# Values, probabilities and p of the first block turned by VectorE in 32x32 squares and placed by DMA, instead of turned by TensorE

## What is computed

```python
hn = rmsnorm(h, norm1[i]);  z = hn @ w_in[i]
u, q, k, v = ...                              # 256 + 3 x 768 features
q, k = rotary(q), rotary(k)                   # 12 heads of 64
# three head groups of 4 heads, dilation 1, 4 and 16, blocks of 128 queries
s = q_block @ k_block(s).T * 64 ** -0.5       # own block and, where there is one, the block before
e = exp(s - max);  o = (e @ v) ...            # the groups' shares are applied later
h = h + concat(pool(u), o) @ w_out[i]
h = h + square(relu(rmsnorm(h, norm2[i]) @ w_up[i])) @ w_down[i]
gate = sigmoid(rmsnorm(h, norm3[i]) @ w_gate[i])
h = h + gate * (p[i] @ w_ple[i])              # p[i]: 1024 tokens x 256
```

## Time and profile before

| | |
|---|---|
| time, median of 3 runs (lowest, highest) | 3045.55 us (3045.34, 3045.76) |
| span of the profiled execution | 3043.6 us |
| PE busy | 3025.0 us, 99% of the span |
| DVE, ACT, POOL busy | 69%, 35%, 64% |
| mean busy share of the 16 DMA engines on queues q1 (SP), q10 (ACT) | 24.0%, 7.3% |

### The profile page before, as it was taken

One profiled execution on the slowest core, in us unless ns is written; L12 is line 12 of the kernel. 1 busy time (PEld: TensorE's weight loads), 2 busy tenths in 40 slices (PEclk: granted clock), 3 DMA queues, 4 the chain that ended last, 5 costly groups with the idle time before them and its releaser, 6 DMA issues.

```text
span 3043.6 us, 40003 instructions
## 1 busy us (share of the span) xinstructions
PE 3025.0 (99%) x14420; PEld 2448.4 (80%) x14420; DVE 2085.4 (69%) x2848; ACT 1057.5 (35%) x1911; POOL 1951.7 (64%) x1630
## 2 busy tenths in 40 slices
PE   8999999999999999999999999999999999999999
PEld 7777888888888888778888888888888777788887
DVE  6656585556888865565665558888769988797223
ACT  4223253333444421233343334444331345302112
POOL 5632458888999557433558878998545544486574
PEclk9999999999999999999999999999999999999999
DMA  5112234446444221112144456544111100111112
GB/s 167 51 42 50 74 108 160 152 153 246 154 152 166 82 84 51 48 43 87 50 140 153 152 187 213 154 148 151 47 44 49 35 28 22 32 49 49 46 63 83
DMA packets 367379, 301.71 MB, mean 99 GB/s; under 512 B 66640, under 2 KB 302160, under 8 KB 365648
## 3 DMA queue, kind: packets, MB, share of 16 engines
q1 hardware_dynamic: 318432, 222.33, 24.0%
q10 hardware_dynamic: 48752, 76.83, 7.3%
HBM read 223.29 MB, written 72.68 MB: 97 GB/s over the span
## 4 chain that ended last, share of the span: by engine, by line
PE 97%; DVE 2%; ACT 0%; issue 0%; DMA 0%; SPq 0%; DVEq 0%; ACTq 0%
PE ring L1581 14%; PE ring L1583 14%; PE ring L1582 14%; PE ring L1862 4%; PE ring L1863 4%; PE ring L1864 4%; PE ring L1895 4%; PE ring L1897 4%; PE ring L1896 4%; PE aux L1581 3%; PE aux L1583 3%; PE aux L1582 3%; PE aux L1895 2%; PE aux L1897 2%; PE aux L1896 2%; PE aux L1862 2%
## 5 line engine op out<-in xcount | busy, mean ns | idle before, releaser
L1288 POOL TENSOR_TENSOR w_hi<-w_raw,ones_r 128x512 fp32r<-128x512 f32 (+3 forms) x296 | 326.4, 1103 | 589.9 <-PE ring L1583 516.5
L1291 POOL TENSOR_TENSOR w_lo<-w_raw,w_hi 128x512 fp32r<-128x512 f32 (+3 forms) x296 | 382.5, 1292 | 23.2
L1581 PE MATMUL ring<-Q_hi,w_hi 128*128 128x512 f32 x752 | 300.1, 399 | 0.0
L1583 PE MATMUL ring<-Q_hi,w_lo 128*128 128x512 f32 x752 | 293.3, 390 | 0.0
L1582 PE MATMUL ring<-Q_lo,w_hi 128*128 128x512 f32 x752 | 293.0, 390 | 0.0
L1581 PE MATMUL ring<-P_hi,w_hi 128*128 128x512 f32 x656 | 268.2, 409 | 1.6 <-DVE P_lo L2716 1.2
L1583 PE MATMUL ring<-P_hi,w_lo 128*128 128x512 f32 x656 | 256.3, 391 | 0.0
L1582 PE MATMUL ring<-P_lo,w_hi 128*128 128x512 f32 x656 | 256.0, 390 | 0.0
L3211 DVE SCALAR_TENSOR_TENSOR conv_out<-conv_in,taps,conv_out 128x1021 f32<-128x1021 f32 (+29 forms) x120 | 188.0, 1614 | 0.2
L1581 PEld LDWEIGHTS ring<-Q_hi,w_hi 128*128 128x128 f32 x752 | 141.1, 188 | 54.0 <-issue 26.3
L1583 PEld LDWEIGHTS ring<-Q_hi,w_lo 128*128 128x128 f32 x752 | 141.2, 188 | 30.2
(11 more groups left out here) (494 smaller groups left out, 8536.5 us busy)
## 6 DMA issues: line engine op xcount, KB each, us to landing
hid_scratch<-stages SPq DMA_DIRECT2D x196, 256.0 KB, 2.1
w_raw<-in_w_in SPq DMA_DIRECT2D x84, 512.0 KB, 3.9
w_raw<-in_w_down SPq DMA_DIRECT2D x64, 512.0 KB, 3.8
p_slot<-hid_scratch ACTq DMA_DIRECT2D x50, 512.0 KB, 4.7
q_slot<-hid_scratch ACTq DMA_DIRECT2D x48, 512.0 KB, 4.7
w_raw<-in_w_up SPq DMA_DIRECT2D x36, 512.0 KB, 4.8
up_raw<-in_w_up SPq DMA_DIRECT2D x28, 512.0 KB, 5.2
p_slot<-first_scratch ACTq DMA_DIRECT2D x12, 1024.0 KB, 7.3
```

What stands on the lines that cost most here:

```text
L1288: g.tensor_tensor(w_hi[:, slot, ks], w_raw[:, slot, ks], one.broadcast_to([P, width, P]), ALU.mult).then_inc(w_hi_ready, 1)
L1291: g.tensor_tensor(w_lo[:, slot, ks], w_raw[:, slot, ks], w_hi[:, slot, ks].bitcast(F32), ALU.subtract).then_inc(w_ready, 1)
L1581: t.matmul(o, wh, xh, start=first, stop=False)
L1583: return t.matmul(o, wl, xh, start=False, stop=last)
```

## The change

VectorE's transpose works on squares of 32x32 only. The change does each transposition in two steps. DVE turns every 32x32 square in place of itself; then DMA puts each square where it belongs.

- Probabilities: `take_scores` and `exp_block` now work in the PSUM banks `turned`. A new job "send" stands five chunks (`SEND_LAG`) behind each step: DVE transposes both banks into `probs` (two instructions of 128x512), and ACT issues one DMA of `probs` (512 KB, rows of 4 KB) to DRAM. At the next step ACT, behind `take_attended` and ahead of `exp_block`, waits for that DMA to land and for `attended` of the stop before, and issues four DMAs (`fetch_probs`), each of 32 partitions by 32 pieces of 32 elements (128 bytes), from DRAM to `probs_t`. PE's `attend` waits for them (`probs_back`).
- Values: DVE transposes `v_feat` in itself (128x1024) where PE's first `turn_v` stood; ACT sends it to DRAM, and at step 0 of the unit, as the first thing, fetches it with four such DMAs to `v_t`.
- p: SP loads it in eight DMAs of 64 KB for each half, again in pieces of 128 bytes, so that the squares stand in the right place before they are turned; DVE transposes 128x512 four times in a layer, in `add_plain`.
- PE's transposes for all three, ACT's copies of v and p and DVE's copies of the probabilities go. Some semaphores are merged.

The core of the diff:

```diff
-STEPS, LAG = 8, 2
+STEPS, LAG, SEND_LAG = 8, 2, 5
+SQUARES = 4
...
-        put(m0, 1, "turn_v", unit, 0)
-        put(m0, 4, "turn_v", unit, 1)
+        put(m0, 1, "turn_v", unit)
...
+            put(m0 + (k + SEND_LAG) // KC, (k + SEND_LAG) % KC, "send", unit, i)
...
     for i in range(stops_of(5) + LAG):
         put_a(8 + 8 * i, "step", 5, i)
+        if i < stops_of(5):
+            put_a(8 + 8 * i + SEND_LAG, "send", 5, i)
...
# SP
-            sp.dma_start(p_raw[:], p_d[l][:, 4 * hf:4 * hf + 4]).then_inc(p_loaded, 16)
+            for i in range(4):
+                for c in range(2):
+                    sp.dma_start(p_raw[32 * i:32 * i + 32, c], p_d[l][hf, c, i]).then_inc(p_loaded, 16)
...
# PE
-            for unit, i in parts:
-                if 1 <= i <= stops_of(unit):
-                    for j in blocks_of(unit, i - 1):
-                        turn_probs(l, unit, j)
...
# PE, attend
-            pe.wait_ge(probs_taken, no + 1)
+            pe.wait_ge(probs_back, 16 * SQUARES * (stops_before(l, unit, j * stops_of(unit) // STEPS) + 1))
...
+            if j == 0:
+                pe.wait_ge(v_back, 16 * SQUARES * (l * UNITS + unit + 1))
...
# ACT
+        def send_v(l, unit):
+            act.wait_ge(v_turned, l * UNITS + unit + 1)
+            act.dma_start(v_d[unit % 2], v_feat[:]).then_inc(v_sent, 16)
+
+        def fetch_v(l, unit):
+
+            act.wait_ge(v_sent, 16 * (l * UNITS + unit + 1))
...
+            squares = v_d[unit % 2].rearrange("(a t) (j b i) -> b t j a i", a=SQUARES, j=8, b=SQUARES)
+            for b in range(SQUARES):
+                act.dma_start(v_t[unit % 2][32 * b:32 * b + 32].rearrange("t j (a i) -> t j a i", a=SQUARES), squares[b]).then_inc(v_back, 16)
...
+        def send_probs(l, unit, i):
+            no = stops_before(l, unit, i)
+            act.wait_ge(probs_turned, step_no(l, unit, blocks_of(unit, i)[-1]) + 1)
+            act.dma_start(probs_d[no % 2], probs[:].rearrange("q x e k -> q (x e k)")).then_inc(probs_sent, 16)
+
+        def fetch_probs(l, unit, i):
+
+            no = stops_before(l, unit, i)
+            act.wait_ge(probs_sent, 16 * (no + 1))
+            act.wait_ge(attended, step_no(l, unit, blocks_of(unit, i)[0]))
+            squares = probs_d[no % 2].rearrange("(a t) (x b j) -> b t x a j", a=SQUARES, b=SQUARES, j=32)
+            for b in range(SQUARES):
+                to = probs_t[32 * b:32 * b + 32].rearrange("t x e k -> t (x e k)").rearrange("t (x a j) -> t x a j", a=SQUARES, j=32)
+                act.dma_start(to, squares[b]).then_inc(probs_back, 16)
+
+        def attention_stop(l, parts):
+            for unit, i in parts:
+                if i >= 2:
+                    for j in blocks_of(unit, i - 2):
+                        take_attended(l, unit, j)
+            for unit, i in parts:
+                if 1 <= i <= stops_of(unit):
+                    fetch_probs(l, unit, i - 1)
+            for unit, i in parts:
+                if i < stops_of(unit):
+                    for j in blocks_of(unit, i):
+                        exp_block(l, unit, j)
...
# DVE
+        def turn_v(l, unit):
+            dve.wait_ge(half_free, half_no(l, 4 + 3 * unit, 1) + 1)
+            v.transpose(v_feat[:], v_feat[:]).then_inc(v_turned, 1)
+
+        def turn_probs(l, unit, i):
+
+            blocks = blocks_of(unit, i)
+            dve.wait_ge(exped, 2 * step_no(l, unit, blocks[-1]) + 2)
+            dve.wait_ge(probs_sent, 16 * stops_before(l, unit, i))
+            for x in range(2):
+                mm = v.transpose(probs[:, x].rearrange("q e k -> q (e k)"), turned[x])
+            mm.then_inc(probs_turned, len(blocks))
...
+        def turn_p(l, c, hf):
+
+            dve.wait_ge(p_loaded, 16 * 8 * (2 * l + hf + 1))
+            if hf:
+                dve.wait_ge(p_ready, p_no(l, c, 0) + 1)
+            v.transpose(p_turned[:, c], p_raw[:, c].rearrange("p j f -> p (j f)")).then_inc(p_copied, 1)
```

More of the change, by code:

```diff
@@ L243, with stops_before @@
 HN3_AFTER = {DOWNS - 4: (0,), DOWNS - 3: (1, 2), DOWNS - 2: (3, 4), DOWNS - 1: (5, 6)}
-STEPS, LAG = 8, 2
+STEPS, LAG, SEND_LAG = 8, 2, 5
+SQUARES = 4
 def stops_of(unit):
     return 2 if unit % GROUPS == 2 else 4
+def stops_before(l, unit, i):
+    return sum(stops_of(u) for u in range(UNITS)) * l + sum(stops_of(u) for u in range(unit)) + i
 def unit_parts(unit, i):
@@ L806, in two_blocks @@
     rooted = sem("rooted")
-    v_taken = sem("v_taken")
+    v_turned = sem("v_turned")
+    v_sent = sem("v_sent")
+    v_back = sem("v_back")
     exped = sem("exped")
-    probs_taken = sem("probs_taken")
+    probs_sent = sem("probs_sent")
+    probs_back = sem("probs_back")
     attn_taken = sem("attn_taken")
@@ L1014, in stat_no @@
         return STATS * l + 2 * i + hf
-    def v_no(l, unit, b):
-        return 2 * (UNITS * l + unit) + b
     def step_no(l, unit, s):
@@ L1497, in _ @@
         for e in range(2):
-            g.memset(left[:, e, 0:1], 1.0).then_inc(left_made, 1)
+            g.memset(left[:, e, 0:1], 1.0).then_inc(keep_made, 1)
         def mask_shares(c, r):
@@ L1638, in sum_split @@
             t.matmul(side, ones_r[:], sum_lo[:, cols], start=False, stop=True).then_inc(side_done, 1)
-        def turn_v(l, unit, b):
-            side_starts(l, "turn_v", unit, b)
-            pe.wait_ge(half_free, half_no(l, 4 + 3 * unit, 1) + 1)
-            for j in range(4):
-                mm = t.transpose(side[:, j * P:j * P + P], v_feat[:, (4 * b + j) * P:(4 * b + j) * P + P], ident[:])
-            mm.then_inc(side_done, 1)
-        def turn_probs(l, unit, j):
-            g, no, (buf, at) = unit % GROUPS, step_no(l, unit, j), buffer_of(unit, j)
-            pe.wait_ge(exped, 2 * no + 2)
-            if stops_of(unit) == 4 and no >= 2:
-                pe.wait_ge(probs_taken, no - 1)
-            elif first_of_stop(unit, j):
-                pe.wait_ge(probs_taken, no)
-            for e in range(2):
-                for b in range(2 if has_prev(g, j) else 1):
-                    mm = t.transpose(turned[buf][:, 256 * e + at + b * P:256 * e + at + b * P + P], probs[:, buf, e, at + b * P:at + b * P + P], ident[:])
-            mm.then_inc(probs_turned, 1)
         def attend(l, unit, j):
@@ L1725, in spread @@
             t.matmul(side, sel[:, g], rows[:], start=True, stop=True).then_inc(side_done, 1)
-        def turn_p(l, c, hf):
-            side_starts(l, "turn_p", c, hf)
-            pe.wait_ge(p_loaded, 16 * (2 * l + hf + 1))
-            for b in range(4):
-                mm = t.transpose(side[:, b * P:b * P + P], p_raw[:, b, c * P:c * P + P], ident[:])
-            mm.then_inc(side_done, 1)
         def woven(l, m, k):
@@ L1940, in _ @@
             turn_x(i)
-        pe.wait_ge(eps_made, 1)
+        pe.wait_ge(ones_made, 2)
         for l in range(DEPTH):
@@ L2251, in exp_block @@
             n, (buf, at) = 2 * P if has_prev(g, j) else P, buffer_of(unit, j)
-            act.wait_ge(max_ready, step_no(l, unit, j) + 1)
+            act.wait_ge(max_ready, step_no(l, unit, j | 1 if stops_of(unit) == 2 else j) + 1)
             for e in range(2):
-                x_ = probs[:, buf, e, at:at + n]
+                x_ = turned[buf][:, 256 * e + at:256 * e + at + n]
                 a.activation(x_, x_, ACT.Exp, scale=SCALE, bias=neg_max[:, j % 4, e:e + 1],
@@ L2312, in woven @@
                 elif kind == "turn_v":
-                    take_v(l, *args)
+                    send_v(l, *args)
                 elif kind == "step":
-                    for part in unit_parts(*args):
-                        attention_stop(l, *part)
+                    if args[1] == 0:
+                        fetch_v(l, args[0])
+                    attention_stop(l, unit_parts(*args))
+                elif kind == "send":
+                    send_probs(l, *args)
                 elif kind == "pool":
@@ L2786, in take_v @@
             if unit and hf == 0:
-                dve.wait_ge(side_done, side_no(l, "turn_v", unit - 1, 1) + 1)
+                dve.wait_ge(v_sent, 16 * (l * UNITS + unit))
             dve.wait_ge(half_done, no + 1)
@@ L2812, in take_scores @@
             dve.wait_ge(attn_consts, l + 1)
+            dve.wait_ge(probs_turned, step_no(l, unit, blocks_of(unit, s * stops_of(unit) // STEPS)[0]))
             dve.wait_ge(scored, step_no(l, unit, last_of_stop(unit, s)) + 1)
             for e in range(2):
-                v.tensor_tensor_reduce(out=probs[:, buf, e, half:half + n], in0=scores[e][:, col:col + n], in1=m, scale=1.0, scalar=-3.0e38,
+                v.tensor_tensor_reduce(out=turned[buf][:, 256 * e + half:256 * e + half + n], in0=scores[e][:, col:col + n], in1=m, scale=1.0, scalar=-3.0e38,
                                        op0=ALU.add, op1=ALU.max, accum_out=row_stat[:, unit, s, e:e + 1]).then_inc(masked, 1)
@@ L2873, in woven @@
                     invert(l, 2, args[0])
+                elif kind == "turn_v":
+                    turn_v(l, *args)
                 elif kind == "step":
```

(5 more changed lines are left out.)

92 lines of the change are left out of this document (27 added, 65 removed).

## The result

The changed kernel takes 3097.7 us (median of four runs, 3096.9 to 3099.4) against 3045.5 us (3045.3 to 3045.8) before: ratio 1.017, 95% interval 1.0158 to 1.0183. Slower by 52 us, where 10 us less had been forecast (3035), and outside the range of 3005 to 3095. The profiled execution has a span of 3095.6 us, so 52.0 more than that of before.

The account below looks back on a forecast made before the run. TensorE, busy 99% of the span, was taken to bound the kernel: span 3043.6 - 48 saved + 37 of waits = 3032.6, plus 1.95 from span to median, about 3035 us; range 3005 to 3095, forecast's own 3017 to 3039.

Parts of the forecast that it names:

- What TensorE saves: Transposes removed from TensorE: 34.0 us for probabilities, 10.4 for v, 3.5 for p, in all 48 us.
- Prices of the loop: ScalarE's way from one `fetch_probs` to the next: issues, exponentials, transposes, send, handing over; 9.0 us against a step of 8.9.
- a sign of being wrong: The prediction said it is wrong if the fetch takes over 7 us, among other signs.
- Rival 2: Fetch too slow: `attend` waits for `probs_back`; 3060 at 1.3 us per DMA, 3130 at 1.8; slower overall had chance 0.34.
- Waits at `attend`: TensorE waiting for the fetched probabilities: 18.5 us per layer, 37 us for two layers, in some 20 waits.
- The last unit and its lag: Each layer's end: about 5.5 us of waits leading into the last unit, 6.1 within it, where steps are 7.5 us apart.
- the walk: Step-by-step timing of a unit of four stops, asking where TensorE waits at `attend`; gave 18.5 us per layer.
- What costs nothing: VectorE's some 21 us more work, p's issues and the shared DMA engines: taken as hidden, with 0 to 2 us possible for p.
- rival 4: TensorE's clock drops to 1.2 GHz behind three waits per layer, some 2 us each: 12 us, 3047; small part of other chances.

Follow-up runs that it names:

- e1: Changed kernel with SyncE's six reloads of hx issued two at a time at three panels instead of six at once: 3098.7 us, ratio 1.0176.
- e13: Changed kernel, two of four DMAs of each probabilities fetch left out from each layer's second unit on, hx reloads two at a time: 3065.6 us.
- e6: Changed kernel with ScalarE's exponentials put ahead of the fetch of the probabilities at a step: 3114.3 us, ratio 1.0224.
- e7: Changed kernel with `attend`, its copy and the fetches moved 4 chunks (2.7 us) behind the step, so behind the exponentials: 3059.6 us, ratio 1.0045.
- e11: Kernel before the change with `attend` and its copy 4 chunks later, transposes still on TensorE, no DMA added: 3140.6 us, ratio 1.0312.
- e3: Kernel before the change with ten pauses of TensorE, each waiting for two chained DMAs, at step 0 of units 1 to 5: 3116.3 us, ratio 1.0233.
- e4: Kernel before the change with twenty pauses of TensorE, one DMA each, at steps 0 and 1 of units 1 to 5: 3107.6 us, ratio 1.0203.

## Why the prediction was wrong, step by step

- **What TensorE saves: right (48).** v and p with the fetch of v in its place gave 14.4 us where 13.9 had been priced. v gave some 12.8 against 10.4. p gave 1.5 against 3.5: the transposes did cost 1.7 per layer, but VectorE's new work for p brought a wait of 0.9 in each, which the prediction had bounded at 0 to 2 us and put at nothing. The probabilities' 34.0 were never measured alone; they stand in the balance of waits, clock and time: 71 + 26 - 48 = 49, measured 52. 3 us are open.
- **Prices of the loop: right on the median.** Transposes 0.717 and 0.674 (forecast 0.7), 1.23 for v (1.2); issues 0.7 (0.6); send 3.2 (2.9). From the first issue of a fetch to its last landing it is 5.4 us in the median of the 40; 5.7 were forecast. But twelve took over 7 us, which I had named as a sign of being wrong: nine behind v's fetch, two in the bursts of reloads, one other.
- **Rival 2, slow pieces of 128 bytes: wrong.** ScalarE's queue has 223,808 packets more than in the earlier trace rows and 0.152 x 16 x 3095.6 - 0.073 x 16 x 3043.6 = 3974 us more: 17.8 ns each, with the 4 KB packets of the sends among them, against 13 forecast for 128 bytes and 29 for rival 2's 3130. The rule that I weighed there (the Trainium skill, page "DMA: Bandwidth & Descriptors", section "Specifications") says that transfers under 512 bytes miss the line rate and are read, changed and written back. The first half agrees with this trace: 128 bytes in 17.8 ns are 7 bytes per ns, where queue q1 before had 698 in 36.7 ns, 19 per ns. The price that I drew from the second half, 26 ns by 13 twice, this trace doesn't show.
- **Waits at `attend`: the sum right by luck, the place not.** 39.7 us in 17 waits, forecast 37 in about 20. The last unit and its lag had been given 11.6 us per layer with what leads into it, 23 in all. Measured at `attend` there are 5.9 and 8.3, 14 in all, and 25.5 elsewhere against the 14 that were forecast. Two errors of some 10 us cancelled. With the waits on v_feat the last units have 19.0 and 13.7.
- **First step that failed, in the order of the prediction: "The fetches share the DMA engines with the weights of a panel (22% busy); a weight load of 1.9 us data in the way would add up to as much to single fetches."** I took the mean of a stretch and one weight load. SyncE's reloads of h and hx, 4 MB at the head of the last unit, are not in that sentence. There the send took 6.1 us and the fetch's DMAs 11.3, and ScalarE was held in its issues for 9.8 us. e1 shows both sides of it: the burst makes the 13 us, and spreading it saves nothing, as the smaller groups meet other fetches. So by itself this step is not what the 52 us hang on. That no fetch there has time to spare, the steps of 7.5 us being shorter than the loop, is how I read e1 and e13.
- **Second, and the largest in us: the other engines in the walk.** "What costs nothing" said of VectorE that "its effect on the order is in the walk", and the walk followed only `attend`. But VectorE waits in order, 101 us in 30 waits for exponentials, and ScalarE's issues stand ahead of `rows`: 31 us of TensorE's waits are for VectorE, in none of my sums. I had named it only under what would make me wrong. e6 shows that these waits and those at `attend` are exchanged for one another when only the order on ScalarE is changed, e7 that both fall when the transfers get more time, and e11 that a wait of VectorE reaches TensorE without any DMA.
- **Third: the clock, nothing in the sum and 12 us in rival 4; it was 26.** The price per wait, 2 us, was right (e3: 21 us over ten). But I counted three waits per layer; where I had 37 us in some 20 waits, there were 71, and waits far shorter than the 3 us that I counted had a half level behind them, one of 1.9 at 255.6 for instance.

In all: the forecast of 3035 holds 37 us of waits; 34 more of waits (31 of them for VectorE) and 26 of clock make 3095, measured 3097.7.

## What to carry to other kernels

Price an issue where it stands in its queue: a wait for a send and four issues of 0.7 us are nothing by busy time, and cost 12 to 14 us here when exponentials stood behind them; moving them behind made of a change without effect a gain of 0.5%. Where a new way of data just fits its step on the mean, look at the shortest step and at the largest burst of transfers in it, and walk through every engine that waits in order, not only through the one that reads the result. And where TensorE never waited, ten waits of 4.4 to 6.2 us cost some 2 us each more than they lasted, and most of 2 us and more had a half clock level behind them, so waits that nearly cancel a gain make a loss.

## What the runs showed of the hardware

- ScalarE's issue of a DMA, 0.7 us for this pattern of 1024 pieces, took 6.4 us at 309.00, when SyncE's queue had the engines at 79%. The exponentials behind it on ScalarE began at 318.9, when the last issue was done.
- A wait for DMA issued from ScalarE's queue grows with what stands ahead in that queue: a fetch in four DMAs took 4.9 to 6.7 us to its last landing in 27 of 30 cases, and 7.2 to 8.9 in nine of ten behind v's four DMAs.
- The added packets, nearly all of 128 bytes, took 17.8 ns each on the mean, the 4 KB ones of the sends included; the line through the two queues of before gives 13 ns for 128 bytes.
- Each turn of TensorE from a product to attention and back cost some 0.2 us beyond the work (0.32 and 0.34 us where a step is 0.23, at 125.0 us in e7).
- TensorE's clock fell to the 1.2 GHz level behind single waits, and not behind all: in e4 behind or at eight of the ten of 2.0 to 4.7 us (not behind one of 3.0 and one of 2.7), and behind none of the ten of 1.6; in the changed kernel behind one of two waits of 1.9 us in the first layer (255.6, not 231.9).
